# Who asks for the filter pieces, and where the first adaLN product and the filter network stand, in a two-layer attention, Hyena and mixture-of-experts step

## What is computed

```python
def adaln(cond, w, b):
    ada = jax.nn.silu(cond) @ w + b            # six vectors a layer: shift, scale, gate, twice

def implicit_filters(L, w1, b1, w2, b2, w3, b3, freq, log_decay):
    hdn = jnp.sin(fr * (feats @ w1 + b1))
    hdn = jnp.sin(fr * (hdn @ w2 + b2))        # the filter network, 64 wide
    filt = hdn @ w3 + b3                       # 4096 taps channels
    filt = filt * jnp.exp(-t_norm * jnp.exp(log_decay)[None, :])
    ...
    return filt / (norm + EPS)

for l in range(DEPTH):
    h = modulate(rmsnorm(x, norm_mix[l]), sh1, sc1)
    x = x + g1 * mixer(h)                      # l = 0 attention, l = 1 Hyena
    h = modulate(rmsnorm(x, norm_ffn[l]), sh2, sc2)
    x = x + g2 * hierarchical_moe(h)
```

## Time and profile before

| | |
|---|---|
| runs, us | 1279.57, 1279.28, 1276.40; median 1279.28 |
| profiled execution | 1278.2 us, span of its instructions 1276.4 us |
| mean granted TensorE clock | 0.932 of full speed |
| busy: TensorE, weight loads | 1094.6 us (86%), 577.4 us |
| busy: VectorE, ScalarE, GpSimd | 470.9, 257.2, 185.9 us |
| DMA | 324.54 MB, mean 254 GB/s over the span |

### The profile page before, as it was taken

The page is one execution under the profiler, slowest core; times in us unless marked ns, Lnnn a source line. Parts: engine busy times, 40 slices in busy tenths (PEclk is TensorE's granted clock), DMA queues, the critical chain, the costliest instruction groups (busy, mean ns, idle before and its releaser), DMA issues.

```text
span 1276.4 us, 14669 instructions
## 1 busy us (share of the span) xinstructions
PE 1094.6 (86%) x5453; PEld 577.4 (45%) x5453; DVE 470.9 (37%) x1002; ACT 257.2 (20%) x498; POOL 185.9 (15%) x209
## 2 busy tenths in 40 slices
PE   5799888987998889999789999989866988778865
PEld 3344555555443334443345565658752422222213
DVE  3356566134233112333363337792440111111116
ACT  3211344022333023323231110000221100000001
POOL 1020000002241113231100002130021222222100
PEclk9899999987999899999889999999877989989987
DMA  9996986432999559999960200505420899999933
GB/s 353 404 325 261 259 322 227 190 132 70 369 395 403 204 212 382 399 402 411 330 236 1 99 1 0 231 0 198 163 92 14 340 414 413 413 412 406 411 144 133
DMA packets 94241, 324.54 MB, mean 254 GB/s; under 512 B 17647, under 2 KB 33423, under 8 KB 77380
## 3 DMA queue, kind: packets, MB, share of 16 engines
q1 hardware_dynamic: 71936, 303.49, 61.4%
q0 software_dynamic: 15504, 13.37, 3.3%
q10 hardware_dynamic: 6708, 6.45, 1.4%
HBM read 333.22 MB, written 30.11 MB: 285 GB/s over the span
## 4 chain that ended last, share of the span: by engine, by line
PE 64%; DMA 19%; DVE 7%; issue 3%; ACT 3%; SPq 3%; POOL 0%; ACTq 0%; POOLq 0%; DVEq 0%
PE bank L844 15%; DMA ring<-in_moe_w_up 10%; PE bank L992 10%; PE bank L858 6%; PE bank L660 3%; PE bank L1031 3%; PE bank L776 3%; DMA ring<-in_w_ada 3%; DMA hT<-in_hy_log_decay 3%; PE bank L563 3%; PE bank L598 2%; PE bank L1020 2%; PE bank L978 2%; DMA ring<-in_moe_w_down 2%; PE bank L791 2%
## 5 line engine op out<-in xcount | busy, mean ns | idle before, releaser
L844 PE MATMUL bank<-ring,work 128*64 128x512 f32 x1120 | 268.9, 636 | 42.4 <-issue 36.3
L844 PEld LDWEIGHTS bank<-ring,work 128*64 128x64 f32 x1120 | 82.7, 146 | 220.0 <-issue 215.8
L858 PE MATMUL bank<-ring,work 128*64 128x512 f32 x560 | 129.2, 604 | 4.2 <-DVE work L1627 1.6
L992 PE MATMUL bank<-hT,ring 128*128 128x384 f32 x384 | 128.0, 494 | 5.3 <-ACT hT L1128 5.3
L1639 DVE SCALAR_TENSOR_TENSOR work<-bank,work 128x256 f32<-128x256 f32 x32 | 15.5, 484 | 261.0 <-ACT work L1224 261.0
L992 PEld LDWEIGHTS bank<-hT,ring 128*128 128x128 f32 x384 | 74.0, 194 | 58.0 <-issue 9.8
L858 PEld LDWEIGHTS bank<-ring,work 128*64 128x64 f32 x560 | 37.5, 138 | 74.0 <-issue 63.3
L1224 ACT ACTIVATE work<-bank 128x256 f32<-128x256 f32 x32 | 12.3, 384 | 247.5 <-PE bank L844 247.5
L1651 DVE COPY work<-bank 128x512 f32<-128x512 f32 x32 | 22.1, 692 | 106.5 <-PE bank L858 106.5
L1788 POOL DMA_INDIRECT work<-token_vectors,work x28 | 28.7, 1026 | 187.2 <-PE bank L827 172.5
L563 PE MATMUL bank<-ring,condS 128*32 128x256 f32 x768 | 47.0, 397 | 8.8 <-DVE ada L1328 5.5
(11 more groups left out here) (263 smaller groups left out, 1505.2 us busy)
## 6 DMA issues: line engine op xcount, KB each, us to landing
ring<-in_moe_w_gate SPq DMA_DIRECT2D x32, 2048.0 KB
ring<-in_moe_w_up SPq DMA_DIRECT2D x32, 2048.0 KB
ring<-in_moe_w_down SPq DMA_DIRECT2D x32, 2048.0 KB
ring<-in_w_ada SPq DMA_DIRECT2D x24, 2048.0 KB, 13.4
ring<-in_hy_w_in SPq DMA_DIRECT2D x6, 2048.0 KB, 19.8
filter_spectra<-work ACTq DMA_DIRECT2D x8, 768.0 KB
work<-expert_rows SPq DMA_DIRECT2D x16, 384.0 KB, 6.6
ring<-filter_spectra SPq DMA_DIRECT2D x2, 3072.0 KB, 12.0
```

The lines of the kernel that those rows point to most:

```text
L844: last = mm(bank[2][WIN * j:WIN * (j + 1), :], gt[:, k, WIN * j:WIN * (j + 1)], gu[:, :, j, k, :], start=(k == 0), stop=(k == KD - 1))
L858: last = mm(bank[b + hf][WIN * j:WIN * (j + 1), :], AT[:, k, WIN * j:WIN * (j + 1)], dn[:, j, k, hf * HALF:(hf + 1) * HALF], start=(k == 0 ...
L992: last = mm(bank[n % 2][:, 0:T], w[:, k, (n % 4) * P:(n % 4 + 1) * P], hT[:, k, :], start=(k == 0), stop=(k == KD - 1))
```

## The change

Three things are edited. First, the rates and the taps weights are no longer asked for by SyncE between the weights of the pairs. ScalarE asks for them on its own queue: rates of piece 0 and taps weights of piece 0 before pair 0, the rates of piece `f + 1` as soon as `decay(f)` has used `eld`, and the taps weights of piece `f` in pair `2f`, behind that. Two DMAs for the two directions become one, so a piece takes three DMAs, not six. Second, adaLN product 0 stands ahead of the square sums; product 1 writes bank 7 and no longer waits for product 0's bank; the small rows are transposed ahead of the tokens. Third, the filter network's two products move from the start to places behind projection blocks 0 and 4 (`MLP_QK`), in bank 3, with their sine arguments and sines.

```diff
@@ -339,10 +339,11 @@
         ADA_QK = {1: 2, 3: 3, 5: 4, 7: 5, 9: 6}
+        MLP_QK = {0: 0, 4: 1}
         ADA_CORE = {0: 7, 2: 8, 4: 9, 5: 10, 7: 11}
...
         QK = 10
-        XT_BANK = [0, 1, 2, 6]
+        XT_BANK = [0, 1, 4, 6]
@@ -380,17 +381,21 @@
-        def load_filter(sp, f):
+        def load_rates(act, f):
             if f >= 1:
-                sp.wait_ge(sem("taps_mm"), 3 * f)
-                sp.wait_ge(sem("dec_set"), 4 * f)
+                act.wait_ge(sem("dec_set"), 4 * f)
             o, n = FILT[f]
-            for d in range(2):
-                lo = (2 * o + d) * D + n * FC
-                sp.dma_start(eld[:, d * FC:(d + 1) * FC], a["hy_log_decay"][0, lo:lo + FC].partition_broadcast(P))\
-                    .then_inc(sem("decay_in"), 16)
-                sp.dma_start(w3c[0:FH, d * FC:(d + 1) * FC], a["hy_filt_w3"][0, :, lo:lo + FC]).then_inc(sem("w3_in"), 16)
-                sp.dma_start(w3c[FH:FH + 1, d * FC:(d + 1) * FC], a["hy_filt_b3"][:, lo:lo + FC]).then_inc(sem("w3_in"), 16)
+            rates = a["hy_log_decay"][0].rearrange("(o d c) -> o d c", o=2, d=2)[o, :, n * FC:(n + 1) * FC]
+            act.dma_start(eld.rearrange("p (d c) -> p d c", d=2), rates.partition_broadcast(P)).then_inc(sem("decay_in"), 16)
+
+        def load_taps(act, f):
+            if f >= 1:
+                act.wait_ge(sem("taps_mm"), 3 * f)
+            o, n = FILT[f]
+            dst = w3c.rearrange("p (d c) -> p d c", d=2)
+            for rows, w in ((slice(0, FH), a["hy_filt_w3"][0]), (slice(FH, FH + 1), a["hy_filt_b3"])):
+                src = w.rearrange("h (o d c) -> h o d c", o=2, d=2)[:, o, :, n * FC:(n + 1) * FC]
+                act.dma_start(dst[rows], src).then_inc(sem("w3_in"), 16)
@@ -407,16 +412,11 @@
             sp.dma_start(hD.rearrange("(c p) d -> p c d", p=P), hTok).then_inc(S_("h_out"), 16)
-            if l == 0:
-                sp.wait_ge(sem("sq_mm"), 2 * KD)
-                load_filter(sp, 0)
             for q in range(2, PAIRS):
...
                 load_dn(sp, l, q)
-                if l == 0 and q % 2 == 1:
-                    load_filter(sp, q // 2)
@@ -531,6 +531,9 @@
             pe.wait_ge(sem("ident_in"), 16)
+            n = R_END - 2 * P
+            pe.wait_ge(sem("early_in"), 16 * (len(early_rows) + 4))
+            tr(bank[7][:, 0:n], prow[0:n, 2, :], ident[0:n, 0:n]).then_inc(sem("pc_mm"), 1)
             pe.wait_ge(sem("x_in"), 16 * TC)
@@ -538,9 +541,6 @@
-            n = R_END - 2 * P
-            pe.wait_ge(sem("early_in"), 16 * (len(early_rows) + 4))
-            tr(bank[7][:, 0:n], prow[0:n, 2, :], ident[0:n, 0:n]).then_inc(sem("pc_mm"), 1)
@@ -548,11 +548,11 @@
-                return bank[2] if t < ADA_CORE[0] else bank[7]
+                return bank[2] if t < ADA_CORE[0] and t != 1 else bank[7]
...
-                if t >= 1:
+                if t >= 2:
@@ -572,7 +572,7 @@
                 if c == 0:
-                    pe.wait_ge(sem("w3_in"), 64 * (f + 1))
+                    pe.wait_ge(sem("w3_in"), 32 * (f + 1))
                     if f >= 1:
@@ -627,18 +627,23 @@
+            pe.wait_ge(sem("cond_set"), 2)
+            ada_mm(0)
             for k in range(KD):
                 norm_sum(0, k)
-            pe.wait_ge(sem("filt_small_in"), 16 * 6)
-            mm(bank[4][0:FH, 0:T], w1, C["feats"][0:FEAT, :], start=True, stop=True).then_inc(sem("mlp_mm"), 1)
-            pe.wait_ge(sem("cond_set"), 2)
-            ada_mm(0)
             ada_tr(0)
-            pe.wait_ge(sem("mlp_done"), 1)
-            pe.wait_ge(sem("pc_done"), 2)
-            mm(bank[5][0:FH, 0:T], w2[:, :], hd1[0:FH, 0, :], start=True, stop=True).then_inc(sem("mlp_mm"), 1)
             ada_mm(1)
             ada_tr(1)
+
+            def mlp(i):
+                if i == 0:
+                    pe.wait_ge(sem("filt_small_in"), 16 * 6)
+                    pe.wait_ge(sem("rt_done"), 1)
+                    mm(bank[3][0:FH, 0:T], w1, C["feats"][0:FEAT, :], start=True, stop=True).then_inc(sem("mlp_mm"), 1)
+                else:
+                    pe.wait_ge(sem("mlp_done"), 1)
+                    mm(bank[3][0:FH, 0:T], w2[:, :], hd1[0:FH, 0, :], start=True, stop=True).then_inc(sem("mlp_mm"), 1)
+
             pe.wait_ge(sem("wkv_in"), 16)
@@ -686,6 +691,8 @@
                     qk_mm(m)
+                if m in MLP_QK:
+                    mlp(MLP_QK[m])
                 if m - 1 in ADA_QK:
@@ -1077,11 +1084,11 @@
-                b = bank[2] if t < ADA_CORE[0] else bank[7]
+                b = bank[2] if t < ADA_CORE[0] and t != 1 else bank[7]
...
-                act.wait_ge(sem("decay_in"), 32 * (f + 1))
+                act.wait_ge(sem("decay_in"), 16 * (f + 1))
@@ -1092,6 +1099,8 @@
                 fn(idle[:, :], eps_col[:, :], ACT.Silu)
+                if f + 1 < NF:
+                    load_rates(act, f + 1)
@@ -1130,8 +1139,6 @@
             for i in range(2):
-                act.wait_ge(sem("angle_set"), i + 1)
-                fn(hd1[0:FH, i, :], hdr[0:FH, i, :], ACT.Sin).then_inc(sem("mlp_done"), 1)
                 adaR_copy(i)
@@ -1144,6 +1151,10 @@
                     adaR_copy(ADA_QK[m])
+                if m in MLP_QK:
+                    i = MLP_QK[m]
+                    act.wait_ge(sem("angle_set"), i + 1)
+                    fn(hd1[0:FH, i, :], hdr[0:FH, i, :], ACT.Sin).then_inc(sem("mlp_done"), 1)
             qk_root(act, fn, QK - 1)
@@ -1215,6 +1226,11 @@
+                if l == 0:
+                    act.wait_ge(S_("htok_set"), B_("htok_set") + 2 * TC)
+                    act.wait_ge(sem("sq_mm"), 2 * KD)
+                    load_rates(act, 0)
+                    load_taps(act, 0)
                 gathered(0)
@@ -1233,6 +1249,7 @@
                         if q >= 2:
+                            load_taps(act, q // 2)
                             store_spectra(q // 2 - 1)
@@ -1288,11 +1305,11 @@
             link(v.memset(minus[0:1, :], 0.0))
+            dve.wait_ge(sem("pc_mm"), 1)
+            v.tensor_copy(pc[:, 2 * P:R_END], bank[7][:, 0:R_END - 2 * P]).then_inc(sem("pc_done"), 1)
             for k in range(KD):
...
                 v.tensor_copy(xT[:, k, :], bank[XT_BANK[k % 4]][:, 0:T]).then_inc(sem("xT_done"), 1)
-            dve.wait_ge(sem("pc_mm"), 1)
-            v.tensor_copy(pc[:, 2 * P:R_END], bank[7][:, 0:R_END - 2 * P]).then_inc(sem("pc_done"), 1)
             dve.wait_ge(sem("pc_mm"), 2)
@@ -1307,7 +1324,7 @@
-                link(v.tensor_scalar(x, bank[4 + i][0:FH, 0:T], fcol[:, i:i + 1], fcol[:, 2:3], ALU.add, ALU.mult))
+                link(v.tensor_scalar(x, bank[3][0:FH, 0:T], fcol[:, i:i + 1], fcol[:, 2:3], ALU.add, ALU.mult))
@@ -1407,10 +1424,8 @@
-            angle(0)
             normalise(0)
             ada_add(0)
-            angle(1)
             ada_add(1)
@@ -1445,6 +1460,8 @@
                     ada_add(ADA_QK[m - 1])
+                if m in MLP_QK:
+                    angle(MLP_QK[m])
             dve.wait_ge(sem("kt_mm"), 1)
```

## The result

The changed kernel takes **1308.22 us**, median of 4 runs (1306.28 to 1309.36), against 1279.32 us for the kernel before (4 runs, 1276.4 to 1279.57). The ratio is 1.0235, with a 95% interval of 1.0219 to 1.0252. The profiled executions have spans of 1307.5 and 1276.4 us, so 31.1 us are to be found in the traces. The forecast was 1289 us (1276 to 1298): the direction was right and the size was less than half.

What follows compares the result with a forecast made beforehand. TensorE was taken to bound the kernel, with DMA close to its limit in the expert pairs. Terms +1.5 - 3.6 + 2.3 + 1.6 + 5.0 + 4.4 = +11.2 us gave 1289 us, range 1276 to 1298.

Steps and rivals of the forecast that it cites:

- pairs 11 and 13: Late expert pairs: weights' queue runs out, so 1.2 us of wait and 1.0 of clock each, +4.4 us (0 to +13).
- pairs 3 and 5 less pair 6: Taps waits of 3 + 2 us in two pairs, less 4.8 and 2.9 us in pair 6: +2.3 us (-3 to +5).
- pair 6 to 7: ScalarE's copy on the chain comes after three more DMA issues, 0.53 us each: +1.6 us.
- pair 9: TensorE waits for the taps weights and then runs at a lower clock: +5.0 us.
- The length of a full wait: Before the taps' matmuls: weights behind the rates land at 513.4 to 514.4, needed at 511.02; 3.0 us (2.4 to 3.4).
- The clock behind a wait: TensorE's work after a taps wait runs at a lower clock: 2.0 us, or 1.0 in pairs 11 and 13.
- Pair 6: A later TensorE finds the down weights there: the 4.8 us wait and 2.9 us of slow running go.
- The rates' waits: ScalarE's waits for the rates in the expert pairs go, as rates are asked for two pairs ahead: -3.6 us.
- The start: Before the pairs: -0.5 + 1.3 + 0.7 = +1.5 us (-4 to +3), with about 5 us of wait before product 2.
- Rival 2: Queue of weights never runs out; five waits of 4 us with 2.5 of clock; 1302.5 us; chance 0.12 including above 1296.
- Rival 1: Taps weights land in time, first packet about 3 us sooner than the store's; 1277.7 us, no change; chance 0.28.
- Rival 3: Faster: taps land in time and adaLN half 5 comes 4 us earlier; -5.3 us, 1272.9 us; chance 0.10.

Runs made afterwards that it cites:

- the kernel with fillers: Changed kernel with four matmuls of unread result on TensorE ahead of the wait for the taps weights, in five filters; 1294.98 us, ratio 1.0142.
- the start alone: Changed kernel's new order of products and filter network, with SyncE's loads as in the kernel before; 1277.69 us, ratio 1.0002.

## Why the prediction fell short, step by step

**The mechanism was right.** The taps weights stand behind the next filter's rates in one queue and miss their use, first in pair 3; the down products after it are slow; ScalarE no longer waits for rates; pair 6 no longer waits for down weights. What failed are sizes. The predicted +9.7 us in the pairs (all terms but the start's) were 27.9. The 18.2 us between them lie in pairs 11 and 13 (+4.4 - 3.6 taken, +7.9 measured), in pairs 3 and 5 less pair 6 (+2.3 taken, +9.1), in pair 6 to 7 (+1.6 taken, +5.6) and in pair 9 (+5.0 taken, +5.5). In the first of these, waits of 6.2 us and slow stretches of 5.1 stand against the 2.4 and 2.0 that I took, since I let the load run beside an emptying queue that was in fact full for most of it.

**The length of a full wait (taken 3.0 us, 2.4 to 3.4).** The waits of pairs 3, 5 and 9 are 3.67, 3.95 and 3.73 us. The chain of the kernel after in pair 3:

```profile
366.21 0.39 ACT L1101
366.60 0.04 issue
366.64 0.69 ACTq L398
367.33 0.03 issue
367.36 9.77 DMA sq<-in_hy_filt_b
377.13 0.04 issue
377.18 3.78 PE bank L581 x4
```

SyncE's queue (q1) and ScalarE's (q10) in 366:370 and in 370:375, then ScalarE's in 375:377:

```profile
q1 hardware_dynamic: 201, 1.30, 78.4%
q10 hardware_dynamic: 12, 0.01, 0.9%
...
q1 hardware_dynamic: 357, 1.45, 74.4%
q10 hardware_dynamic: 377, 0.37, 21.7%
...
q10 hardware_dynamic: 327, 0.32, 45.4%
```

The rates are issued at 366.22 and their first packet starts at 369.76, after 3.5 us. The 4.1 us read from the store were close, a little too long; by the packet records that store's first packet started 3.8 us after its issue. Then 377 packets go in 5 us, 75 a us, beside 357 of SyncE's: the equal turns and the 79 a us held too. By 375.0 the queue has moved 389, yet TensorE goes on at 377.18. The step that failed is "up to 1 us to completion" behind the 386th piece. The load has 420 packets. The queue has moved as many by 375.26, but by the packet records the load's last four-byte packet, the 34th, is at 376.63, and TensorE starts 0.55 us later. I read from this that some of the 420 were already the store, on engines that were through with their share, while others still had pieces of the load; the records don't name the engine. From the rates' issue to TensorE it is 10.0 to 11.3 us in the five pairs, where I had 9.6 to 10.6 in the full ones.

**Pairs 11 and 13 (taken 1.2 us each).** The waits are 3.56 and 2.68 us, and this is the larger miss in length. The weights' queue does thin out, but too late. In pair 10 to 11, in 564:568 and 568:569:

```profile
q1 hardware_dynamic: 268, 1.09, 69.4%
q10 hardware_dynamic: 295, 0.30, 21.2%
...
q10 hardware_dynamic: 195, 0.18, 53.9%
q1 hardware_dynamic: 52, 0.18, 48.0%
```

For 4 of the 5 us the queues still take equal turns; only in the last one does ScalarE's run at 195 a us. I had let the emptier queue work over the whole load and taken the 229 a us of the earlier trace rows. The load's last packet is 6.2 us behind its first in pair 11 and 5.4 in pair 13, against 6.9 in pair 3: 0.7 and 1.5 us are saved, not 2. The waits sum to 17.6 us, predicted 11.4.

**The clock behind a wait (taken 2.0 us, and 1.0 in the late pairs).** Less its wait, an odd pair is longer than the 14.77 us of an undisturbed one by 3.3 us in pair 3, 1.8 in pair 9, 3.4 in pair 11 and 1.7 in pair 13; in pair 5 the sum over its rows is 3.4. That makes 13.6 us, where I had 8; the kernel with fillers, which has no such stretches, recovers 12.0. I had weighed 1.35 us behind a wait of 1.26 against 2.9 behind one of 4.8, but both count one product alone. Here the taps (+1.9 us), the transposes (+0.7) and the down product (+0.8) all run in the slow stretch.

**Pair 6 (taken -7.7 us).** Pair 5 has a wait of 3.95 us and 3.4 of slow clock, and the stretch to pair 6 is 2.1 us longer, so 5.3 us come back. The wait for down weights is gone (4.8), but of the 2.9 us of slow gate/up only 1.4: that product now follows an idle stretch of 2.42 us behind VectorE and takes 8.55 us, against 9.96 before and 7.09 at full speed. Another 0.9 us of the gain goes with that idle stretch. Pairs 3 and 5 less pair 6: +9.1, predicted +2.3.

**Pair 6 to 7 (taken +1.6 us).** It is +5.6. ScalarE after, and TensorE before and after, in this order:

```profile
466.23 0.39 ACTq L389 DMA_DIRECT2D hT<-in_hy_log_decay  x1
466.66 0.68 ACTq L398 DMA_DIRECT2D sq<-in_hy_filt_w  x1
467.37 1.14 ACTq L398 DMA_DIRECT2D sq<-in_hy_filt_b  x1
467.51 0.20 ACT L1101 ACTIVATE idle<-eps_col 128x1 f32<-128x1 f32 x1
468.60 0.58 ACTq L1119 DMA_DIRECT2D filter_spectra<-work  x1
471.27 0.60 ACT L1222 ACTIVATE work<-bank 128x512 f32<-128x512 f32 x1 [3.56 <-issue]
```

```profile
456.20 7.09 PE L844 MATMUL bank<-ring,work 128*64 128x512 f32 x32 [1.50 <-ACT work L1211]
```

```profile
471.92 9.08 PE L851 MATMUL bank<-ring,work 128*64 128x512 f32 x32 [5.07 <-ACT work L1222]
```

I had given every issue the store's 0.53 us. The three take 0.39, 0.68 and 1.14 us, and the whole way from the exponentials to the copy is 5.1 us instead of 2.0; TensorE's idle time grows by 3.6, and its next product is 2.0 us longer behind it. The kernel that asks for the taps weights first issues them beside the exponentials, and there TensorE's idle time is 3.00 us. The other kernels say the same: this stretch is 34.9 us with the start alone, 37.6 to 38.1 in the kernels whose ScalarE asks for the pieces but without a wait, and 40.4 in the change.

**The rates' waits (taken -3.6 us).** Pair 13 had 18.21 us in place of 14.77 and pair 11 14.92: 3.6 us, as predicted, though nearly all in pair 13 and not 1.0 of it elsewhere, so the sum is right partly by luck. In the kernels that lose nothing by the taps, pair 13 still takes 15.3 to 16.5 us: TensorE has a gap of 0.49 to 1.63 us before pair 14's gate/up, where it had 0.41 before. I take it to wait for that pair's weights, which no run here tried. So 1.7 to 2.9 us are gained in pair 13.

**The start (taken +1.5 us).** Up to 126 us the two traces end alike. The chain of the kernel after:

```profile
43.44 8.30 PE bank L658 x16
51.74 0.78 PE bank L642 x2
52.53 5.36 PE bank L658 x16
57.88 3.59 PE bank L563 x64
```

The wait of 5 us that I placed before product 2 isn't there. The first projection starts at 43.44, 2.1 us earlier than before and not 3 to 4, and takes 8.30 us at a granted clock of 0.64. So TensorE comes to product 2 only at 57.88; neither half keeps it waiting then, and product 2 runs at full speed, without the +1.3 us, and is done at 61.5, before the 62 us that I had named. The early product did win 0.8 us by the second pair of projections (62.32 against 63.13), and the second product of the filter network, 0.79 us, took it back. The +3.1 us before pair 0 come from stretches between 165 and 300 us whose matmuls the change leaves as they were. With the same start and other loads, pair 0's gate/up began at 310.5 to 314.7 us in the kernels above, and with the start of before at 309.4 to 313.3. Whether the +3.1 are an effect of the change stays open. From 275 to 310 us the granted clock is 0.56 in the changed kernel and in six of the seven others that have both its start and its ScalarE loads, and 0.66 in the remaining one, in the kernel before and in the three with only one of the two. No time shows a loss by it: the three measurements at 0.56 without waits are at 1276 us.

**The rivals.** Rival 2, at 1302.5 us, came nearest in size and wasn't what happened: the queue of weights did run out in the late pairs. Its five waits of 4 us with 2.5 of clock are close to the measured 3.5 and 2.7. Rival 1 asked for a load that leaves 3 us sooner than a store. By the packet records loads left 3.5 to 3.8 us after their issue and the stores of the kernel before, from pair 2 to pair 12, 3.8 to 4.0. The time that it gave for taps that land in time, 1277.7 us, is near what the kernels with the better order took (1276), by other terms: nothing at the start and about 3 us in pair 6 to 7. Rival 3 is ruled out: product 2 was done at 61.5 us.

## What to carry over

A small transfer in a shared queue ended later than the mean rate of the queue said. I would count its end from the first request ahead of it, which was 10 to 11 us here for 420 small packets beside a full queue. Put first in a queue what is needed first: the rates were wanted two pairs later and the taps weights 7 us later, and exchanging the two was worth some 30 us. A short idle stretch of TensorE cost more than its length here; price all the work that follows it, not one product, and look for the engine whose sequencer issues DMAs between two steps of a chain.

## What the runs showed of the chip

- An idle stretch of TensorE of 2.7 to 4.0 us was followed by a lower granted clock (0.68 over the next 10.6 us in pair 3) and cost another 1.7 to 3.4 us. With the stretch filled by matmuls whose result is thrown away, the kernel was some 12 us faster (ratios 1.0142 and 1.0235 to the kernel before).
- The issue of a DMA on ScalarE took 0.39 us for the rates (128 partitions), 0.68 for `w3` (64 partitions) and 1.14 for `b3`, which is one partition with two pieces: the smallest transfer had the longest issue. In pairs 4 and 12 `w3`'s took 1.59 us.
- A load puts more packets into its queue than it has pieces: 34 of 420 packets carry 4 bytes.
- A first packet left 3.5 to 3.8 us after its issue began in all five pairs, with SyncE's queue full beside it. Ahead of pair 0 of the changed kernel the same request left after 1.9 us (issue at 297.23, first packet at 299.14); no DMA had moved anything for 13 us before SyncE's first packet at 298.12. The Trainium skill ("DMA: Bandwidth & Descriptors", Specifications) has 0.6 us to the first byte; neither place shows so little, and the measured times decide.
